# Moving the argument and intermediate of the inverse square roots, and of the preparation's small chains, from SBUF into the PSUM tile of the sums

## The reference

```python
def rmsnorm(x, g):
    y = xf * lax.rsqrt(jnp.mean(xf * xf, axis=-1, keepdims=True) + RMS_EPS)

# gated delta rule, per head, chunks of 64 positions
q = _l2norm(q) * (A_DK ** -0.5);  k = _l2norm(k)
diff = G[..., :, None] - G[..., None, :]
decay = jnp.where(incl, jnp.exp(jnp.where(incl, diff, 0.0)), 0.0)
L = jnp.where(strict, beta[..., :, None] * kk * decay, 0.0)
sol = lax.linalg.triangular_solve(eye + L, rhs, lower=True, unit_diagonal=True)
p_intra = einsum("bhncd,bhnjd->bhncj", q, k) * decay
```

## Time and profile before

| | |
|---|---|
| median of 3 runs | 2648.89 us (2648.45 to 2652.58) |
| profiled execution, device time | 2641.71 us |
| its span, first to last instruction | 2640.4 us |
| PE / PEld busy | 2534.7 / 2082.8 us |
| DVE, ACT, POOL busy | 1091.0, 952.4, 1171.0 us |
| mean granted TensorE clock | 0.985 of full speed |

### The profile page before, as it was taken

How to read it: one execution, slowest core, us unless ns; L and a number is a source line. 1 busy time by engine, 2 the same in 40 slices (tenths; PEclk the granted TensorE clock), 3 DMA queues, 4 the chain that set the end, 5 groups by cost and what they waited for, 6 DMA issues and landing times.

```text
span 2640.4 us, 32470 instructions
## 1 busy us (share of the span) xinstructions
PE 2534.7 (96%) x12760; PEld 2082.8 (79%) x12760; DVE 1091.0 (41%) x2281; ACT 952.4 (36%) x1448; POOL 1171.0 (44%) x1565
## 2 busy tenths in 40 slices
PE   7999999999999999998999999999999999999998
PEld 5777888888777888886888878877777887888886
DVE  6965111125964111126657765413445523311112
ACT  4553322234553222234434333324553344321221
POOL 5114665653115665654323121433324654665653
PEclk9999999999999999999999999999999999999999
DMA  4442222225522323223111101132212232222222
GB/s 160 128 109 80 96 82 102 97 87 143 144 81 82 108 79 107 91 85 114 62 49 49 49 33 49 49 112 93 84 65 96 97 112 80 96 86 98 96 91 77
DMA packets 41367, 237.27 MB, mean 90 GB/s; under 512 B 4736, under 2 KB 5888, under 8 KB 18560
## 3 DMA queue, kind: packets, MB, share of 16 engines
q1 hardware_dynamic: 38912, 218.43, 23.8%
q0 software_dynamic: 2304, 16.78, 3.1%
HBM read 214.22 MB, written 4.19 MB: 83 GB/s over the span
## 4 chain that ended last, share of the span: by engine, by line
PE 82%; DVE 11%; ACT 3%; POOL 2%; issue 1%; DMA 1%; SPq 0%; DVEq 0%; ACTq 0%; POOLq 0%
PE PB L1750 67%; PE PB L1786 3%; PE PB L1752 3%; POOL WL L2789 2%; DVE cc L2404 1%; PE PB L1770 1%; PE PB L1938 1%; PE PB L1957 1%; PE PB L1762 1%; ACT WH L2002 1%; PE PB L1945 1%; PE PB L1822 1%; PE PB L1781 1%; DVE NEWT L2281 1%; DVE NEWT L2279 1%
## 5 line engine op out<-in xcount | busy, mean ns | idle before, releaser
L2789 POOL TENSOR_TENSOR WL<-WR,WH 128x256 fp32r<-128x256 f32 (+1 forms) x1444 | 1042.9, 759 | 901.0 <-ACT WH L2002 901.0
L1750 PE MATMUL PB<-HH,WH 128*128 128x512 f32 x1992 | 806.7, 405 | 12.7 <-ACT HH L2017 9.9
L1750 PE MATMUL PB<-HL,WH 128*128 128x512 f32 x1992 | 783.6, 393 | 1.9 <-DVE HL L2300 1.9
L1750 PE MATMUL PB<-HH,WL 128*128 128x512 f32 x1992 | 519.2, 396 | 0.3 <-POOL WL L2789 0.3
L1750 PEld LDWEIGHTS PB<-HH,WH 128*128 128x128 f32 x1992 | 378.7, 190 | 104.4 <-issue 15.8
L2002 ACT ACTIVATE WH<-WR 128x2048 fp32r<-128x2048 f32 (+1 forms) x209 | 371.6, 1778 | 229.5 <-PE PB L1750 223.0
L1750 PEld LDWEIGHTS PB<-HL,WH 128*128 128x128 f32 x1992 | 378.4, 190 | 80.6 <-issue 4.8
L1750 PEld LDWEIGHTS PB<-HH,WL 128*128 128x128 f32 x1992 | 366.5, 189 | 73.7 <-issue 3.4
L1750 PE MATMUL PB<-BL,WH 128*128 128x512 f32 x848 | 332.4, 392 | 0.8 <-DVE BL L2309 0.8
L1750 PE MATMUL PB<-BH,WH 128*128 128x512 f32 x784 | 309.5, 395 | 2.7 <-ACT BH L2031 2.7
L2315 DVE TENSOR_TENSOR X<-X,PB 128x512 f32<-128x512 f32 x80 | 55.0, 687 | 354.2 <-PE PB L1750 354.2
(11 more groups left out here) (344 smaller groups left out, 2991.1 us busy)
## 6 DMA issues: line engine op xcount, KB each, us to landing
WR<-in_w_gu SPq DMA_DIRECT2D x66, 1024.0 KB, 4.8
WR<-in_w_dn SPq DMA_DIRECT2D x48, 704.0 KB, 4.0
WR<-in_w_in SPq DMA_DIRECT2D x22, 1024.0 KB, 4.8
WL<-WR POOLq DMA_DIRECT2D x16, 1024.0 KB, 7.0
WR<-in_qkv SPq DMA_DIRECT2D x12, 1024.0 KB, 4.8
WR<-in_w_out SPq DMA_DIRECT2D x8, 1024.0 KB, 4.8
WR<-in_qk SPq DMA_DIRECT2D x8, 1024.0 KB, 4.8
WR<-in_gb SPq DMA_DIRECT2D x4, 1024.0 KB, 4.8
```

The lines of the kernel that those rows point to most:

```text
L1750: ins = pe.matmul(out[:, 0:n], wt[:, k * cols + j * P:k * cols + (j + 1) * P], x[:, k, 0:n], start=first, stop=last)
L2789: ins = g.tensor_tensor(m.WL[u % 2][:, part], m.WR[u % 2][:, part], f32(m.WH[u % 2][:, part]), ALU.subtract)
```

## The change

`newton` gets x and y from its caller. They lie now in columns 480 to 495 of the very bank that holds the sums (`roots_in`), in PSUM, while the result stays in SBUF. Within a round the order of the products is changed, so that every instruction has at most one tensor input from SBUF: y = (x * -0.5) * col, y = y * col, col = (y + 1.5) * col. The number of instructions is the same. `rs2` keeps one 4-column helper in SBUF (NEWT, now 128x4).

In `p4` the subtraction writes back into the `prow` 0 bank instead of DT, the masking reads the bank and writes DT, the small factors lie in that bank's columns 480 to 491, and a wait for the masking stands ahead of them. The bank is freed after L2594's operation (`pdn`) instead of after the first subtraction (`p4a`). `p6` uses the `prow` 2 bank, waits for its last reader (`pel`), and the bank is freed after `p6` (`psq`) instead of after `p15`.

```diff
-            room.free(at("p4a", h))
+            room.free(at("pdn", h))
...
-            room2.free(at("pel", h))
             cfree[f"q{i}"] = [t.done, at("pqd", h), at("p1q", h)]
-            step("p6", h)
+            step("p6", h, tile=t2)
+            room2.free(at("psq", h))
...
-    def newton(n, col):
-        x, y = m.NEWT[:, 0:n], m.NEWT[:, 8:8 + n]
+    def newton(x, y, col):
...
         for i in range(3):
             dv.wait()
-            dv.link(v.tensor_tensor(y, col, col, ALU.mult))
+            dv.link(v.scalar_tensor_tensor(y, x, -0.5, col, ALU.mult, ALU.mult))
             dv.wait()
-            dv.link(v.scalar_tensor_tensor(y, y, -0.5, x, ALU.mult, ALU.mult))
+            dv.link(v.tensor_tensor(y, y, col, ALU.mult))
             dv.wait()
             ins = v.scalar_tensor_tensor(col, y, 1.5, col, ALU.add, ALU.mult)
...
+    def roots_in(bank, n):
+        return bank[:, 480:480 + n], bank[:, 488:488 + n]
...
-            v.tensor_tensor(v4(m.DT[:]), v4(PB[w["tile"].b][:]), m.RC[:, :, 0, h:h + 1].broadcast_to([P, 4, P]), ALU.subtract).then_inc(sems["p4a"], 1)
+            bank = PB[w["tile"].b]
+            x, y = roots_in(bank, 4)
+            v.tensor_tensor(v4(bank[:]), v4(bank[:]), m.RC[:, :, 0, h:h + 1].broadcast_to([P, 4, P]), ALU.subtract).then_inc(sems["p4a"], 1)
             ve.wait_ge(*at("p4a", h))
-            v.tensor_tensor(v4(m.DT[:]), v4(m.DT[:]), over_blocks(m.CON[:, C_INCL:C_INCL + P]), ALU.add).then_inc(sems["p4"], 1)
+            v.tensor_tensor(v4(m.DT[:]), v4(bank[:]), over_blocks(m.CON[:, C_INCL:C_INCL + P]), ALU.add).then_inc(sems["p4"], 1)
+            ve.wait_ge(*at("p4", h))
             ve.wait_ge(*at("pks", h))
-            dv.link(v.tensor_scalar(norms(h, 1), norms(h, 0), 1e-6, None, ALU.add))
+            dv.link(v.tensor_scalar(x, norms(h, 0), 1e-6, None, ALU.add))
             dv.wait()
-            dv.link(v.reciprocal(norms(h, 1), norms(h, 1)))
+            dv.link(v.reciprocal(x, x))
             dv.wait()
-            dv.link(v.tensor_tensor(norms(h, 1), norms(h, 1), m.RC[:, :, 1, h], ALU.mult))
+            dv.link(v.tensor_tensor(y, x, m.RC[:, :, 1, h], ALU.mult))
             dv.wait()
-            v.tensor_tensor(norms(h, 3), norms(h, 1), m.RC[:, :, 3, h], ALU.mult).then_inc(sems["pkn"], 1)
+            v.tensor_tensor(norms(h, 3), y, m.RC[:, :, 3, h], ALU.mult).then_inc(sems["pkn"], 1)
...
-            v.tensor_tensor(v4(m.DT[:]), v4(m.DT[:]), norms(h, 1).unsqueeze(2).broadcast_to([P, 4, P]), ALU.mult).then_inc(sems["pdn"], 1)
+            v.tensor_tensor(v4(m.DT[:]), v4(m.DT[:]), y.unsqueeze(2).broadcast_to([P, 4, P]), ALU.mult).then_inc(sems["pdn"], 1)
...
-            x, r = m.NEWT[:, 0:4], m.l2c[:, 0:4]
+            r = m.l2c[:, 0:4]
+            x, y = roots_in(PB[w["tile"].b], 4)
+            ve.wait_ge(*at("pel", h))
             dv.link(v.tensor_scalar(x, norms(h, 0), 1e-6, None, ALU.add))
-            dv.link(newton(4, r))
+            dv.link(newton(x, y, r))
```

More of the change, by code:

```diff
@@ L130, in memory @@
     m.SMALL = sb("SMALL", [P, 256])
-    m.NEWT = sb("NEWT", [P, 16])
+    m.NEWT = sb("NEWT", [P, 4])
     g0 = cur[0]
@@ L2320, in vector_program @@
             n, j0 = w["n"], w["j0"]
+            bank = PB[w["tile"].b]
+            x, y = roots_in(bank, n)
             ve.wait_ge(*w["tile"].done)
@@ L2323, in vector_program @@
             if w["extra"] is not None:
-                dv.link(v.scalar_tensor_tensor(m.NEWT[:, 0:n], PB[w["tile"].b][:, j0:j0 + n], w["scale"], w["extra"], ALU.mult, ALU.add))
+                dv.link(v.scalar_tensor_tensor(x, bank[:, j0:j0 + n], w["scale"], w["extra"], ALU.mult, ALU.add))
             elif w["sums"] is None:
-                dv.link(v.tensor_scalar(m.NEWT[:, 0:n], PB[w["tile"].b][:, j0:j0 + n], w["scale"], w["eps"], ALU.mult, ALU.add))
+                dv.link(v.tensor_scalar(x, bank[:, j0:j0 + n], w["scale"], w["eps"], ALU.mult, ALU.add))
             else:
@@ L2329, in vector_program @@
                 dv.wait()
-                dv.link(v.scalar_tensor_tensor(m.NEWT[:, 0:n], PB[w["tile"].b][:, j0:j0 + n], w["scale"], w["sums"], ALU.mult, ALU.add))
-            newton(n, w["col"]).then_inc(sems["rsqrt"], 1)
+                dv.link(v.scalar_tensor_tensor(x, bank[:, j0:j0 + n], w["scale"], w["sums"], ALU.mult, ALU.add))
+            newton(x, y, w["col"]).then_inc(sems["rsqrt"], 1)
         elif kind == "diag":
@@ L2507, in vector_program @@
             bank = PB[w["tile"].b]
-            v1, v2 = m.NEWT[:, 0:4], m.NEWT[:, 4:8]
+            x, y = roots_in(bank, 8)
+            v1, v2 = x[:, 0:4], x[:, 4:8]
             ve.wait_ge(*w["tile"].done)
             ve.all(w["after"])
+            dv.link(v.tensor_scalar(m.NEWT[:], bank[:, 0:4], 1e-6 / D, 1e-12, ALU.mult, ALU.add))
             dv.link(v.tensor_scalar(v1, bank[:, 0:4], 1.0 / D, 1e-6, ALU.mult, ALU.add))
-            dv.link(v.tensor_scalar(v2, bank[:, 4:8], 1.0 / D, None, ALU.mult))
             dv.wait()
-            dv.link(v.scalar_tensor_tensor(v2, v1, 1e-6, v2, ALU.mult, ALU.add))
-            dv.link(newton(8, m.l2c[:]))
+            dv.link(v.scalar_tensor_tensor(v2, bank[:, 4:8], 1.0 / D, m.NEWT[:], ALU.mult, ALU.add))
+            dv.link(newton(x, y, m.l2c[:]))
             dv.wait()
```

## The result

| | before | after |
|---|---|---|
| median of 4 runs each | 2650.73 us (2648.45 to 2652.85) | 2617.60 us (2613.51 to 2621.84) |
| ratio after / before | | 0.9875, 95% interval 0.9856 to 0.9894 |
| profiled execution, device time | 2641.71 us | 2616.85 us |
| its span | 2640.4 us | 2615.6 us |
| its mean granted TensorE clock | 0.985 | 0.989 |

The change is worth 33 us by the medians and 25 us by the two profiled executions; 18 were forecast. The direction and the mechanism of the waits held.

The account below looks back on a forecast made before the run. PE bounds it, busy 2534.7 of 2640.4 us. Gains 14.6 + 3.4 - 0.4 + 3 = 20.6 us, less 2.8, give 18; off the 2648.9 median that makes 2631 us, range 2618 to 2644.

Parts of the forecast that it names:

- The mechanism: In the roots, instructions with at most one SBUF input no longer wait for POOL's pieces: 0.65 against 0.16 us.
- Still wait for POOL: Rival, chance 0.06: in the roots a PSUM operand does not free instructions from POOL; nothing changes, 2649 us.
- slow PSUM write: Rival, chance 0.08: a link writing PSUM takes 0.30 us in roots and small chains; gain 10, 2639 us.
- The waits as a sum: 14.6 us behind roots plus 3.4 in preparation, less 0.4 for added waits and 2.8 for new POOL meetings.
- 2097: PE's STAT wait at 2097.19 us, behind the root from 2088.60: all 0.71 us go.
- `rs2`: 4.04 booked: Start of the delta rule: root shrinks from 7.94 to 3.0 us, STAT then 1.4; PE's whole 4.04 us wait goes.
- the -2.8: Taken back: about 4 new POOL meetings of two-SBUF-input DVE operations that stood behind slow roots, 0.70 us each.
- Preparation: Chain before each head's inversion shortens: 1.2 us each for heads 1 and 6, 0.5 each for 0 and 3.
- The clock: Granted clock behind head 5's and `rs2`'s waits: 4.0 and 0.4 us lost, 3 of 4.4 taken as gain.
- Moves on: Rival, chance 0.17: freed DVE instructions meet the same POOL pieces; half the waits, no clock; gain 9, 2640 us.
- More than booked: Rival, chance 0.11: all 4.9 us of `rs2` pass through, later inversion waits shrink, whole clock returns; 28 us, 2621.
- Slower: Rival, chance 0.06: holding `prow` 2's bank longer reorders delta-rule lanes; 3 us in each of 8 heads, 2655 us.

## Why the prediction was right in kind and short in size

- *The mechanism* of the waits was right, and only this one. With the same instructions in SBUF the gain is 5 us of 30, and without POOL's bursts none that can be told. "Still wait for POOL" and "slow PSUM write" fall: 0.17 us a link, 10 ns for the write instead of the 0.1 us of the rival. The Trainium skill's rule (SBUF — State Buffer, Who interferes with whom) carried over: fewer SBUF inputs, no meeting.
- *The waits as a sum* were right: 14.6 + 3.4 - 0.4 - 2.8 = 14.8 forecast, 14.5 measured over all executions and 15.2 between the two traces. Its terms were not all right, and their errors cancelled, so the closeness is in part luck.
  - Head 5: 4.01 booked, 3.7 found.
  - 205, 1585 and 1719: 5.86 booked, 5.86 found.
  - 2097: 0.71 booked, 0.10 found. The root is 3 us shorter, but the two operations HL between it and STAT (two SBUF inputs each) now take 1.31 and 1.22 us where they took about 0.7, and STAT 1.22 where it took 0.68, in a burst. I had not looked at what stands between the root and STAT on DVE.
  - `rs2`: 4.04 booked, 3.33 found at the wait, since the sum took the two copies in front of STAT at their clean length, and they stood in the burst. Against it 2.05 came back at `pad`. This belongs to the -2.8, but it is no meeting with POOL: the fixed 14.66 us between the two `pad` waits took it.
  - Preparation: 1.2 us each for heads 1 and 6, found 1.13 and 1.23; head 0 0.86 where 0.5 was booked; all waits for inversions 3.9 where 3.4 was booked.
  - Not booked: the wait at 719.65, 2.41 us, now 0.67. A root ahead of it had an instruction of 2.10 us (at 713.63, beside POOL's DMA and its rotary product, not its splitting); I looked for waits for STAT and YY, directly behind a root, and this one is for a square sum queued behind the root.
- *The clock* is the step that failed. I took 3 us of the 4.4 that the trace of before showed behind two waits. Measured are 15.2 over all executions, and 10.8 between the two traces. Two faults: I read the clock at two places only, though the page's mean of 0.985 says that 39.6 us were lost in the whole span (from 1205 to 1300 alone 6.7, of which I booked 0.4, and from 700 to 830 another 3.9, of which I booked none); and I read it in one execution, whose clock term of 39.6 is below the mean of 47.8 over 77 executions. Taking the gain off the median of 2648.9 was right in form, but the sum was then a mix, waits of one execution that are stable and a clock that is not. Booked at the size of the waits, the clock would have made the sum 14.8 + 15 = 30, and 2619, but nothing known then gave that size.
- *The place where most was gained for a wait*: head 5's `p6`. Its kernel gains 9.4 us (standard error 1.8) for a wait of 4.01. The rows show 7.9 of it, 3.8 of wait and 4.1 of clock. Whether the rest is more than spread is left open, since the later stretches differ from execution to execution.
- *Rivals.* "Moves on" happened in part (STAT 691 to 1150 ns, the copies, HL). What STAT's part of it cost was 2.5 us of rest, by the kernel that reads the column from PSUM, not the 9 that this rival takes off the gain. "More than booked" gave the nearest time, 2621, by the wrong path: the waits for inversions fell by 3.9 us, not by 10.9, and the clock did the rest. "Slower" fell: the later releases cost nothing (1.0004).
- *What should show it* came as said for the links, for `rs2`, for the wait on YY and for the clock after head 5; the STAT waits came to 9.6 where 8.0 was said.

## What to carry to other kernels

Where DVE works on a few columns while POOL streams through SBUF, give each DVE instruction a PSUM operand in a tile that it holds anyway: 0.65 us become 0.17. Before adding up waits, work out (1 - mean clock) x span for several executions. Here it was half as large as the waits, and a us of wait taken away on a busy TensorE was worth 0.2 to 2.3 us: it depended on the place, not on the length of the wait. Ask also what sets the time behind a wait. Where a chain on another engine has a fixed length, as between the two `pad` waits, a faster PE only waits longer for it. Changing one of several like places alone understated the whole here, 22.2 us against 29.7.

## What the runs showed of the hardware that was not expected

- The same program with the same waits (96.8 and 97.1 us) ran with 39.6 and 55.7 us of clock term. Behind the same wait of 3.23 us the mean clock was 1.00 in one execution and 0.80 in the other.
- Waits differ in what they give back when taken away: 9.4 us for head 5's 4.01, 6.5 for the memory's 3.23, 9.2 for the norms' 7.6 together, 0.6 for `rs2`'s 3.3 (standard errors 0.9 to 1.8).
- For the same 48 products between the two `pad` waits PE took 13.27 us at a granted clock of 0.83 and 11.22 us at 1.00, and the second wait was 1.39 us in the one and 3.44 in the other.
- A 128x4 DVE instruction takes 161 ns with a PSUM input and an SBUF output, 170 ns with a PSUM output, and about 162 ns with all in SBUF and no burst beside it.
- STAT, 128x512, with a diagonal mask and a broadcast column both in SBUF, took 1150 ns on average in the 8 products from RCOL, 691 ns there with POOL's bursts shortened, and 683 ns with the column in PSUM.
- Instructions with one SBUF input and an SBUF output waited too beside POOL: L2275 0.64 us, the two copies of 4 columns 0.65 and 0.78 us.
